# A delta-rule stage on pairs of heads: the identity added on VectorE, products spread over four array tiles, activation tables loaded at chosen places

## The chip, the core and the metric

The kernel runs on one core of one Trainium2 chip. The metric is the device time of one execution in microseconds (us), lower is better. TensorE (PE) does the matrix products and writes PSUM (eight banks of 128 partitions x 512 fp32), VectorE (DVE) and ScalarE (ACT) read PSUM, GpSimd (POOL) works on SBUF alone. Each engine has its own instruction queue; they meet at semaphores.

## The reference, cut to what matters

Two networks run one after the other: a two-layer block (Fourier mixing, then an RWKV-7 style mixer, each followed by an expert-choice mixture of experts) and a two-layer transformer. The change is about the RWKV scan of the first block (16 heads of 64, 512 tokens and 256 context tokens, forward and backward), and about where functions of ScalarE are used in all of the program.

```python
def wkv_scan(r, decay, k, v, a_vec, b_vec, s0, reverse):
    def step(s, inp):
        r_t, w_t, k_t, v_t, a_t, b_t = inp
        sa = jnp.einsum('bhvk,bhk->bhv', s, a_t)
        s = s * w_t[:, :, None, :] + sa[..., None] * b_t[:, :, None, :] + v_t[..., None] * k_t[:, :, None, :]
        return s, jnp.einsum('bhvk,bhk->bhv', s, r_t)
```

Around it: `a = sigmoid(...)`, `kk * rsqrt(sum(kk*kk) + 1e-12)`, `rsqrt(var + LNX_EPS)`, and in the norms `rsqrt(mean(h*h) + eps)`. The kernel writes each reciprocal root as Exp(-0.5 Ln(x)).

## The kernel before, in words

**The stage.** The heads are taken in eight pairs (`p`); a pair has two halves, one for each direction `d`. The 768 tokens are 12 chunks of 64 (`CH`), in three groups of four (`GC`, index `b`). Head one of the pair lies on partitions 0 to 63, head two on 64 to 127. `heads2` (line 1355) issues a product of 64x64 matrices for both heads; with `across=True` the result of each head goes to the other head's half of the partitions.

**The levels.** In every chunk the inverse of a triangular matrix is needed. It is doubled up in five levels. `X` holds the inverse so far and `XT` its transpose, side by side in one tile `XX`; POOL makes `NL`, the part of the triangular matrix that belongs to the level (line 3170). A level is: on TensorE `T` = product of `NL` and `X` (`level_t`, line 1433), which ScalarE copies to SBUF (`copied`, line 2046, all at line 2049); on TensorE the double product `XT`'`T` and `T`'`XT` into the two halves of one bank (`level_x`, line 1441); on VectorE X + (double product), 512 columns wide (`level`, line 2669, instruction at line 2675; in the last level only `XT`, line 2677).

**Beside the levels** runs what belongs to the other direction: a `chain` of 11 steps (named z; TensorE line 1450, VectorE line 2684) that carries the state from chunk to chunk, and on VectorE the preparation of the next half: a scan along the tokens (line 2691, and for one direction 2694), the keys (2700, 2705, 2707, 2710 or 2712), decays (2717, 2718, 2723, 2724, 2728), and for the output of the pair before 2748, 2753, 2759, 2764. ScalarE has the sigmoids (2068, 2069), the square (2059) and the scaling (2074) of the keys, Ln of the key sums (2079), the Exps (2089, 2098, 2114 to 2117). The sums over a head's channels (named kn, var, bonus) and the gate are 128-wide products at line 895.

**What sets the order.** Four lists, `RK_PE`, `RK_DVE`, `RK_ACT`, `RK_POOL`, name the steps of a pair in the order in which each engine does them; each finished step adds one to the engine's semaphore. `RK_READ` says which bank a step's result lies in and which step empties it. `banks` (line 1365) makes TensorE wait for the reader of the bank's last content. The loops of all four engines are written out in the same order. After the levels a half ends with scores, transposes, the products with the inverse and the chunk products (sb, sk, wu, ba, kt, ar, kv, bc, y), some of them with `across` products alternating with straight ones.

**Function tables.** ScalarE evaluates Ln, Exp, Sigmoid and Silu from tables that `ACT_TABLE_LOAD` brings in. The kernel of before leaves the loads to the compiler, which puts one ahead of each function whose table isn't in. `root` (line 1915, Ln at 1920, Exp at 1923) is used by every norm of the program.

Of the kernel before, what the change touches and what calls it, by code (L numbers as in the profile page):

```python
# [28 lines left out]
KT = D // 128  # L29
# [68 lines left out]
for _d in range(2):  # L98
# [4 lines left out]
    RK_PE += [("mv", _d, _b) for _b in range(3)] + [("kn", 0), ("kn", 1)] * _d  # L103
# [13 lines left out]
    for _l in range(1, 6):  # L117
        for _b in range(3):
            RK_DVE += [("XX", _d, _l, _b)] + [_z.pop(0) for _ in range(min(1, len(_z)))]
        RK_DVE += {1: [("scan", _a)] + [("kkn",)] * _d, 2: [("kdk", _a), ("bdk", _a), ("ksm", _a)] + [("yn",)] * _d,  # L120
                   3: [("ara", _a), ("arr", _a)],
                   4: [("bds", _a), ("kds", _a)] + ([("res1",), ("lnx",)] if _d else [("ksr",)]),
                   5: [("res",), ("bonus",)] * _d + [("mt", _a, 0)]}[_l]
# [5 lines left out]
    RK_ACT += [("mv", _d, _b) for _b in range(3)] + [("ka", _a)]  # L129
    for _l in range(1, 6):  # L130
        RK_ACT += [("T", _d, _l, _b) for _b in range(3)]
        RK_ACT += {1: [("kn", 0), ("kn", 1), ("var",), ("kr",), ("rs",)] * _d, 2: [("exps", _a)], 3: [("aff",)] * _d}.get(_l, [])
# [5 lines left out]

RK_READ = {}
_xx, _t, _a4 = 0, 0, 0  # L140
for _name in RK_PE:
# [4 lines left out]
    elif _k in ("x0", "XX"):  # L146
        RK_READ[_name] = {_xx % 2: [("dve", _name)]}
        _xx += 1
    elif _k in ("mv", "T"):
        RK_READ[_name] = {2 + _t % 2: [("act", _name)]}  # L150
        _t += 1
    elif _k == "z":
        RK_READ[_name] = {6: [("dve", _name)]} if _rest[1] < 11 else {}
        if _rest[1] == GC:
            RK_READ[_name][7] = [("dve", ("yf", _rest[0]))]
    elif _k in ("vt", "kn", "var", "bonus", "gate"):
        RK_READ[_name] = {4 + _a4 % 2: {"gate": [("dve", ("res",))], "bonus": [("dve", ("bonus",))]}.get(_k, [("act", _name)])}
        _a4 += 1
    elif _k == "mean":
        RK_READ[_name] = {0: [("dve", ("cen",))]}  # L160
    elif _k == "kv":
        RK_READ[_name] = {(1, 3, 4)[_rest[1]]: [("dve", ("bc",) + _rest)]}
        if _rest[1]:
            RK_READ[_name][(None, 2, 5)[_rest[1]]] = [("dve", ("y",) + _rest)]
    elif _k in ("bc", "y"):
        RK_READ[_name] = {}
    else:
        _bank = {"sb": (4, 4, 4), "sk": (5, 5, 5), "ba": (6, 6, 6), "kt": (7, 7, 7), "wu": (2, 3, 2), "ar": (0, 0, 1)}[_k][_rest[1]]
        RK_READ[_name] = {_bank: {"sb": [("act", ("nt",) + _rest)], "sk": [("dve", ("mt",) + _rest)], "ar": [("dve", _name)]}.get(_k, [("act", _name)])}
# [226 lines left out]
def build(nc, slabs_d, vecs_d, tabs1_d, tabs2_d, aux_d, lora_d, x_d, ctx_d, out_d, kv_d):  # L396
# [5 lines left out]
    with stack:  # L402
# [15 lines left out]
        P = [stack.enter_context(nc.psum_tensor(f"bank{i}", [128, 512], f32)) for i in range(8)]  # L418
# [471 lines left out]
        def _(pe):  # L890
# [474 lines left out]
            def banks(p, *name, after=()):  # L1365
# [3 lines left out]
                         if not (front and (step[0] in ("bonus", "res") or engine == "act" and step in RK_ACT[:RK_ACT.index(("pw", 0))])) and not (back and step[0] != "z")]  # L1369
# [63 lines left out]
            def level_t(p, d, l):  # L1433

                for b in range(3):
                    out, = banks(p, "T", d, l, b, after=[("pool", 0, "nl", d, l, b), ("dve", 0, "XX", d, l - 1, b) if l > 1 else ("dve", 0, "x0", d, b)])
                    for q, c in enumerate(chunks(b)):
                        m = heads2(out[:, q * CH:(q + 1) * CH], NL[:, c, :], X[:, c, :])
                    m.then_inc(rk_pe, rk.one("T", d, l, b))
# [43 lines left out]
            def inverse_times(p, d, b):  # L1483

                out, = banks(p, "wu", d, b, after=[("dve", 0, "XX", d, 5, b), ("act", 0, "mv", d, b)])
# [58 lines left out]
            for p in range(KT):  # L1544
                for d in range(2):
# [7 lines left out]
                    if d == 1:  # L1553
                        key_sums(p)
                    for l in range(1, 6):
                        level_t(p, d, l)
                        for b in range(3):
                            level_x(p, d, l, b)
                            if 3 * l + b < NCH + 2:
                                chain(p, a, 3 * l + b - 2)  # L1560
                        if (d, l) == (1, 1):
                            head_sums(p, "var", sqs, "act", ("sq",))
                            head_sums(p, "bonus", ksr, "dve", ("ksr",))
                        if (d, l) == (1, 2):
                            gate_product(p)
# [1841 lines left out]
```

## Time and profile before

| | us |
|---|---|
| median of 3 runs | 4458.05 |
| the runs | 4448.03 to 4460.98 |
| the profiled execution | 4450.12 |
| its span, first to last instruction | 4448.3 |
| of it the eight pairs (1227.8 to 2142) | 914 |

The share of the span that an engine is busy is an average over stages with different limits. The eight pairs are the stretch that the change is about; the rows that matter are taken from there, from one pair whose halves are 1345.3 to 1396.8 and 1396.8 to 1460.2 us. An instruction for TensorE of this program is two in the trace, since a product of fp32 matrices is made in two passes: a group of eight products is x16 there.

### The profile page before, as it was taken

What the parts mean: (1) busy time and instruction counts of PE and PEld (TensorE: products, weight loads), DVE (VectorE), ACT (ScalarE), POOL (GpSimd) and SP (SyncE); (2) the same over time, 40 slices, a digit from 0 to 9 for tenths busy, and PEclk for the clock granted to TensorE, in tenths of its full rate; (3) what the DMA queues carried; (4) which work ended last, traced back from release to release, by engine and by line L of the source; (5) the groups of instructions that cost most, each with busy time, mean ns of one, the idle gap of its engine ahead of it and who ended that gap; (6) DMA issues with size and microseconds to landing.
All of it is one profiled execution on the core that took longest, in us unless ns stands there. A gap on an engine that the chain in (4) does not pass through costs nothing.

```text
span 4448.3 us, 93542 instructions
## 1 busy us (share of the span) xinstructions
PE 4030.2 (91%) x40040; PEld 2621.0 (59%) x40040; DVE 1730.7 (39%) x3445; ACT 870.8 (20%) x1893; POOL 659.4 (15%) x603
## 2 busy tenths in 40 slices
PE   5989999989888888888879998999999989999998
PEld 4534444455477777777434443447588854657887
DVE  2412121164555555555231222354345424515353
ACT  2200000020144444444110001215000011330001
POOL 4000000000033333323000000000234300003342
PEclk8989999999999999999889999999999999999999
DMA  7387878832100000000249997110122221102221
GB/s 325 127 313 300 336 299 333 331 160 89 60 12 12 12 10 11 12 12 12 119 186 429 429 428 329 57 57 1 57 78 93 76 73 49 39 20 76 95 76 38
DMA packets 54241, 619.72 MB, mean 139 GB/s; under 512 B 5648, under 2 KB 8976, under 8 KB 18320
## 3 DMA queue, kind: packets, MB, share of 16 engines
q1 hardware_dynamic: 49664, 599.41, 34.1%
q10 hardware_dynamic: 2448, 9.05, 0.5%
q0 software_dynamic: 1792, 6.29, 0.4%
q8 instruction: 271, 4.44, 0.4%
q14 instruction: 66, 0.54, 0.0%
HBM read 602.40 MB, written 12.32 MB: 138 GB/s over the span
## 4 chain that ended last, share of the span: by engine, by line
PE 70%; issue 14%; DVE 6%; DMA 5%; ACT 1%; DVEq 1%; PEld 1%; PEldq 0%; SPq 0%; POOLq 0%; ACTq 0%; POOL 0%
PE bank L895 56%; PE bank L1358 13%; DMA ring<-slabs 3%; DMA work<-slabs 2%; DVE work L2675 1%; PEld bank L895 1%; DMA kv<-work 1%; PE bank L1405 1%; DVE hx L2367 0%; PEldq L1796 0%; DVE work L3049 0%; DVE work L2723 0%; DVE work L2724 0%; DVE work L2352 0%; DVE work L2343 0%
## 5 line engine op out<-in xcount | busy, mean ns | idle before, releaser
L895 PE MATMUL bank<-ring,work 128*32 128x256 f32 (+3 forms) x7002 | 764.4, 439 | 68.6 <-DMA ring<-slabs 56.7
L895 PE MATMUL bank<-work 128*128 128x256 f32 (+8 forms) x3590 | 783.0, 428 | 26.6 <-DVE work L3049 15.9
L895 PEld LDWEIGHTS bank<-work 128*128 128x128 f32 (+3 forms) x3590 | 498.2, 184 | 300.0 <-issue 219.5
L895 PEld LDWEIGHTS bank<-ring,work 128*32 128x32 f32 (+2 forms) x7002 | 317.2, 124 | 490.8 <-issue 387.1
L895 PE MATMUL bank<-work,ring 128*128 128x256 f32 (+1 forms) x1616 | 482.2, 456 | 14.7 <-DVE work L3068 5.1
L895 PE MATMUL bank<-hx,ring 128*128 128x512 f32 (+1 forms) x1344 | 485.7, 516 | 9.2 <-DVE hx L2367 7.3
L1358 PE MATMUL bank<-work 64*64 64x64 f32 x11520 | 419.5, 224 | 82.0 <-issue 62.6
L1358 PEld LDWEIGHTS bank<-work 64*64 64x64 f32 x11520 | 385.5, 139 | 118.2 <-issue 117.1
L895 PEld LDWEIGHTS bank<-work,ring 128*128 128x128 f32 x1616 | 306.6, 191 | 184.4 <-issue 134.4
L895 PEld LDWEIGHTS bank<-hx,ring 128*128 128x128 f32 x1344 | 257.1, 192 | 224.1 <-issue 200.4
L3186 POOL TENSOR_TENSOR work<-ring 128x512 f32<-128x512 f32 (+1 forms) x48 | 78.7, 1640 | 1938.0 <-DVE resc L3037 1490.2
L3170 POOL TENSOR_TENSOR work<-work,tabs_sb 128x256 f32<-128x256 f32 x288 | 226.0, 803 | 363.8 <-ACT work L2049 279.9
L2343 DVE TENSOR_TENSOR work<-work,bank 128x256 f32<-128x256 f32 x240 | 91.8, 416 | 405.7 <-ACT work L2321 402.2
L2049 ACT ACTIVATE work<-bank 128x256 f32<-128x256 f32 (+1 forms) x355 | 145.1, 416 | 372.8 <-PE bank L1358 367.7
L2675 DVE TENSOR_TENSOR work<-work,bank 128x512 f32<-128x512 f32 x192 | 131.4, 685 | 182.9 <-PE bank L1358 181.7
L2321 ACT ACTIVATE work<-bank 128x256 f32<-128x256 f32 x48 | 18.4, 383 | 735.0 <-PE bank L895 735.0
L1358 PE MATMUL bank<-ring,work 64*64 64x64 f32 (+1 forms) x3168 | 119.3, 258 | 40.6 <-issue 16.5
L895 PE MATMUL bank<-work,tabs_sb 128*128 128x512 f32 (+1 forms) x276 | 129.6, 598 | 14.5 <-ACT work L1907 9.5
L2560 DVE TENSOR_TENSOR work<-work,bank 128x256 f32<-128x256 f32 x16 | 6.8, 422 | 323.3 <-PE bank L895 323.3
L3049 DVE SCALAR_TENSOR_TENSOR work<-work 128x256 f32<-128x256 f32 x176 | 124.4, 722 | 14.7 <-issue 5.2
L1358 PEld LDWEIGHTS bank<-ring,work 64*64 64x64 f32 x3168 | 102.9, 144 | 46.2 <-issue 45.5
L895 PE MATMUL bank<-resc,work 128*128 128x256 f32 x512 | 121.3, 380 | 3.1 <-POOL work L3186 2.6
(315 smaller groups left out, 4621.8 us busy)
## 6 DMA issues: line engine op xcount, KB each, us to landing
ring<-slabs SPq DMA_DIRECT2D x228, 2048.0 KB, 9.7
work<-slabs SPq DMA_DIRECT2D x48, 2048.0 KB, 18.3
work<-kv SPq DMA_DIRECT2D x18, 384.0 KB, 3.0
kv<-work SPq DMA_DIRECT2D x2, 3072.0 KB, 15.7
kv<-work ACTq DMA_DIRECT2D x6, 512.0 KB, 17.2
work<-tabs ACTq DMA_DIRECT2D x1, 2176.0 KB, 9.5
resx<-xT SPq DMA_DIRECT2D x1, 2048.0 KB, 10.8
outT<-hx ACTq DMA_DIRECT2D x8, 256.0 KB, 2.6
```

What stands on the lines that cost most here:

```text
L895: return pe.matmul(out, lhsT, rhs, start=(k == 0), stop=(k == n - 1))
L1358: m = pe.matmul(out[other if across else r], lhsT[r], rhs[r], start=first, stop=last)
L1405: pe.matmul(outw[:, 0:n], wa2[two[d], 0:128], HW[two[d], at:at + n], start=True, stop=True)
L2049: act.activation(dst, src, ACT.Copy).then_inc(rk_act, rk.next(*name))
L2321: act.activation(keep1, ff_result(n, "p1"), ACT.Copy).then_inc(ff_act, 1)
L2343: v.tensor_tensor(out, a, b, op)
L2560: v.tensor_tensor(hidc, gactc[:, h, :], ex_bank(l, f"u{h}c")[:, 0:256], ALU.mult)
L2675: v.tensor_tensor(XX[:, :, cs_, :], XX[:, :, cs_, :], p4, ALU.add).then_inc(rk_dve, rk.one("XX", d, l, b))
L3049: return v.scalar_tensor_tensor(dst, x, 1.0, y, ALU.mult, ALU.subtract)
L3170: m = pool.tensor_tensor(NL[:, cs_, :], NT[d][:, cs_, :], mask, ALU.mult)
L3186: pool.tensor_tensor(s3, a["a11"], a["a21"], ALU.subtract).then_inc(ff_pool, 1)
```

## The change

1. **Levels.** VectorE adds the identity to `T` as it takes it out of PSUM (256 columns). The double product is then the new `X` and `XT` itself, not what is to be added, and ScalarE copies it out, both halves in one instruction of 512 columns. The two halves of the double product lie in two banks (a pair of banks 0 and 1, or 4 and 5), and one of the two products is issued `across`, so that they go to different array tiles.
2. **Order within a level.** Before: T0 T1 T2, XX0 z XX1 z XX2 z. After: T0 T1 z T2, XX0 z XX1 XX2 z on TensorE, and T0 T1 z T2 z (first part of the other work) z (second part) on VectorE.
3. **Other places.** The sums kn and var stand ahead of level 1, gate and bonus behind level 4. Ln of the keys and of the variance stands ahead of the level loop; the scaling of the keys stands behind level 1.
4. **Tables.** `preload_act_table_set` names a set with both Ln and Exp, and sets for sigmoid and for silu, at chosen places.
5. **Banks.** A new table `RK_BANK`, and one PSUM tensor for all eight banks, so that one instruction can read two.

```diff
-    for _l in range(1, 6):
-        RK_PE += [("T", _d, _l, _b) for _b in range(3)]
-        for _b in range(3):
-            RK_PE += [("XX", _d, _l, _b)] + [_z.pop(0) for _ in range(min(1, len(_z)))]
-        RK_PE += {1: [("var",), ("bonus",)], 2: [("gate",)]}.get(_l, []) * _d
+    for _l in range(1, 6):
+        RK_PE += [("T", _d, _l, 0), ("T", _d, _l, 1)] + [_z.pop(0) for _ in range(min(1, len(_z)))] + [("T", _d, _l, 2)]
+        RK_PE += [("XX", _d, _l, 0)] + [_z.pop(0) for _ in range(min(1, len(_z)))] + [("XX", _d, _l, 1), ("XX", _d, _l, 2)]
+        RK_PE += [_z.pop(0) for _ in range(min(1, len(_z)))]
+        RK_PE += [("gate",), ("bonus",)] * (_d == 1 and _l == 4)
...
+    elif _k == "XX":
+        _pair = 4 * (_rest[2] % 2)
+        RK_READ[_name] = {_pair: [("act", _name)], _pair + 1: [("act", _name)]} if _rest[1] < 5 else {(0, 4, 1)[_rest[2]]: [("act", _name)]}
...
-                out, = banks(p, "XX", d, l, b, after=[("act", 0, "T", d, l, b)])
+                outs = banks(p, "XX", d, l, b, after=[("dve", 0, "T", d, l, b)])
                 for q, c in enumerate(chunks(b)):
                     if l < 5:
-                        heads2(out[:, q * CH:(q + 1) * CH], XT[:, c, :], T[d][:, c, :])
-                    m = heads2(out[:, 256 + q * CH:256 + (q + 1) * CH], T[d][:, c, :], XT[:, c, :])
+                        heads2(outs[0][:, q * CH:(q + 1) * CH], XT[:, c, :], T[d][:, c, :], across=l > 1)
+                    m = heads2(outs[-1][:, q * CH:(q + 1) * CH], T[d][:, c, :], XT[:, c, :], across=l in (1, 5))
...
+            def level_copy(p, d, l, b):
+
+                cs_ = slice(GC * b, GC * b + GC)
+                if l < 5:
+                    pair = list(RK_READ["XX", d, l, b])[0]
+                    copied(p, XX[:, :, cs_, :], PB[:, pair:pair + 2, 0:256].rearrange("p x (c n) -> p x c n", c=GC), "XX", d, l, b)
+                else:
+                    copied(p, XT[:, cs_, :], ONE(rk_bank("XX", d, l, b)[:, 0:256]), "XX", d, l, b)
...
-                v.wait_ge(*rk_done("pe", p, "XX", d, l, b))
-                p4 = rk_bank("XX", d, l, b)[:, :].rearrange("p (x c n) -> p x c n", x=2, c=GC)
-                cs_ = slice(GC * b, GC * b + GC)
-                if l < 5:
-                    v.tensor_tensor(XX[:, :, cs_, :], XX[:, :, cs_, :], p4, ALU.add).then_inc(rk_dve, rk.one("XX", d, l, b))
-                else:
-                    v.tensor_tensor(XT[:, cs_, :], XT[:, cs_, :], p4[:, 1, :, :], ALU.add).then_inc(rk_dve, rk.one("XX", d, l, b))
+                v.wait_ge(*rk_done("pe", p, "T", d, l, b))
+                v.tensor_tensor(T[d][:, GC * b:GC * b + GC, :], rk_bank("T", d, l, b)[:, 0:256].rearrange(CHUNKED, c=GC),
+                                bc(eye2.unsqueeze(1), 128, GC, CH), ALU.add).then_inc(rk_dve, rk.one("T", d, l, b))
...
                     for b in range(3):
                         copied(p, AM[d][:, GC * b:GC * b + GC, CH:128], ONE(rk_bank("mv", d, b)[:, 0:256]), "mv", d, b)
-                    key_factors(p, a)
+                    act.preload_act_table_set("natural_log_exp_and_others")
+                    if d == 1:
+                        key_logs(p)
+                        variance_logs(p)
...
+                    if p < KT - 1 or d == 0:
+                        act.preload_act_table_set("sigmoid_and_others")
```

The order on TensorE, first in one level of a half (behind the first T groups of level 2; `resc` and `work` are the chain's operands, x2 the two products of a z step, `work` alone T and XX). Before:

```order
L1358 MATMUL bank<-work 64x64 x40
L1358 MATMUL bank<-resc,work 64x64 x2
L1358 MATMUL bank<-work,resc 64x64 x2
L1358 MATMUL bank<-work 64x64 x16
L1358 MATMUL bank<-resc,work 64x64 x2
L1358 MATMUL bank<-work,resc 64x64 x2
L1358 MATMUL bank<-work 64x64 x16
```

After:

```order
L1353 MATMUL bank<-work 64x64 x16
L1353 MATMUL bank<-resc,work 64x64 x2
L1353 MATMUL bank<-work,resc 64x64 x2
L1353 MATMUL bank<-work 64x64 x24
L1353 MATMUL bank<-resc,work 64x64 x2
L1353 MATMUL bank<-work,resc 64x64 x2
L1353 MATMUL bank<-work 64x64 x32
```

The first z step stands between the second and the third T group now, and the last two double products stand together.

VectorE in levels 1 and 2 of a second half (`d` = 1). Before:

```order
L2675 TENSOR_TENSOR work<-work,bank 128x2x256
L2684 SCALAR_TENSOR_TENSOR work<-bank,work,hc 128x64
L2691 SCALAR_TENSOR_TENSOR work<-tabs_sb,work 128x780
L2700 SCALAR_TENSOR_TENSOR work<-work 128x768
L2675 TENSOR_TENSOR work<-work,bank 128x2x256
L2684 SCALAR_TENSOR_TENSOR work<-bank,work,hc 128x64
```

After:

```order
L2694 TENSOR_TENSOR work<-bank,tabs_sb 128x256
L2702 SCALAR_TENSOR_TENSOR work<-bank,work,hc 128x64
L2709 SCALAR_TENSOR_TENSOR work<-tabs_sb,work 128x780
L2702 SCALAR_TENSOR_TENSOR work<-bank,work,hc 128x64
L2718 SCALAR_TENSOR_TENSOR work<-work 128x768
L2694 TENSOR_TENSOR work<-bank,tabs_sb 128x256 x2
```

The 512-wide additions have become 256-wide ones, and a chain step stands between the two parts of the other work.

ScalarE at the start of the same half, from the copies of mv on. Before:

```order
L2049 ACTIVATE ring<-bank 128x4x64 x3
L2074 ACTIVATE work<-work 128x768
L2049 ACTIVATE work<-bank 128x256 x3
L2079 ACT_TABLE_LOAD
L2079 ACTIVATE work<-bank,work 128x256
L2079 ACTIVATE work<-bank,work 128x512 x2
L2089 ACT_TABLE_LOAD
L2089 ACTIVATE work<-work 128x768
L2098 ACTIVATE work<-work 128x512
L2049 ACTIVATE work<-bank 128x256 x3
```

After:

```order
L2054 ACTIVATE ring<-bank 128x4x64 x3
L2172 ACT_TABLE_LOAD
L2084 ACTIVATE work<-bank,work 128x256
L2084 ACTIVATE work<-bank,work 128x512 x2
L2054 ACTIVATE work<-bank 128x2x256 x3
L2079 ACTIVATE work<-work 128x768
L2094 ACTIVATE work<-work 128x768
L2103 ACTIVATE work<-work 128x512
L2054 ACTIVATE work<-bank 128x2x256 x3
```

The load and the three Lns stand ahead of the level's first copies, the second load is gone, and the copies are 512 wide.

## Rows read from the trace of the kernel before

**Rows 1.** Page, part 1: engine, busy us, share, instructions.

```profile
PE 4030.2 (91%) x40040; PEld 2621.0 (59%) x40040; DVE 1730.7 (39%) x3445; ACT 870.8 (20%) x1893; POOL 659.4 (15%) x603
```

**Rows 2.** Windows of two halves and five pairs: length, busy us by engine, clock.

```profile
1345.30:1396.80 51.50, 43.99 (x1382) 40.11 (x1378) 30.30 (x60) 20.73 (x44) 17.85 (x24) 1.00 0.05 14
1396.80:1460.20 63.40, 52.00 (x1438) 45.90 (x1434) 30.96 (x60) 27.03 (x53) 16.34 (x24) 0.95 0.03 10
1460.20:2031.50 571.30, 477.24 (x14064) 429.56 (x14060) 304.87 (x600) 239.16 (x486) 171.71 (x231) 0.96 0.04 12
```

**Rows 3.** Timeline of TensorE, first half: start, duration, tiles, idle before.

```profile
1348.93 0.98 PE L1358 MATMUL bank<-work 64*64 64x64 f32 x32 [1.48 <-issue]
...
1377.76 0.27 PE L1358 MATMUL bank<-ring,work 64*64 64x64 f32 x2
```

**Rows 4.** Timeline of TensorE, second half.

```profile
1403.39 2.83 PE L1358 MATMUL bank<-work 64*64 64x64 f32 x80
...
1413.78 2.70 PE L1358 MATMUL bank<-work 64*64 64x64 f32 x48 [1.83 <-issue]
...
1435.64 0.68 PE L1358 MATMUL bank<-work 64*64 64x64 f32 x16 [1.01 <-DVE work L2677]
1438.13 1.18 PE L1358 MATMUL bank<-ring,work 64*64 64x64 f32 x27 [1.80 <-DVE work L2764]
```

**Rows 5.** TensorE: a z product, a double product, and straight with across alternating.

```profile
1423.36 0.31 PE L1358 MATMUL bank<-work,hc 64*64 64x64 f32 x4
1423.48 1.13 PE L1358 MATMUL bank<-work 64*64 64x64 f32 x32
...
1391.32 0.69 PE L1358 MATMUL bank<-work,hx 64*64 64x64 f32 x32 [1.42 <-issue]
```

**Rows 6.** Groups of instructions of the eight pairs: busy us, mean ns, idle before.

```profile
L2675 DVE TENSOR_TENSOR work<-work,bank 128x512 f32<-128x512 f32 x192 | 131.4, 685 | 182.9 <-PE bank L1358 181.7
L2684 DVE SCALAR_TENSOR_TENSOR work<-bank,work,hc 128x64 f32<-128x64 f32 x80 | 22.2, 278 | 0.7 <-PE bank L1358 0.7
L2666 DVE TENSOR_TENSOR work<-bank,tabs_sb 128x256 f32<-128x256 f32 x47 | 19.9, 424 | 34.2 <-PE bank L1358 33.6
L2707 DVE TENSOR_TENSOR work<-work 128x768 f32<-128x768 f32 x16 | 18.8, 1175 | 0.0
L2705 DVE TENSOR_TENSOR work<-work 128x768 f32<-128x768 f32 x16 | 15.2, 948 | 0.0
```

**Rows 7.** VectorE's other work in levels 1 to 4, by half.

```profile
1356.14:1359.10 2.96, 2.89 (x4) 1.00 0.02 6
1362.63:1365.87 3.24, 3.24 (x5) 1.00 0.00 0
1369.11:1371.02 1.91, 1.91 (x3) 1.00 0.00 0
1374.38:1376.79 2.41, 2.41 (x5) 1.00 0.04 7
...
1420.12:1423.70 3.58, 3.58 (x6) 1.00 0.02 5
1426.93:1428.97 2.04, 2.00 (x3) 1.00 0.04 8
1432.68:1435.08 2.40, 2.40 (x5) 1.00 0.03 7
```

**Rows 8.** Timeline of ScalarE: two loads of a table, one 512-wide copy.

```profile
1345.26 1.28 ACT L2068 ACT_TABLE_LOAD   x1 [1.00 <-PE bank L1406]
...
1410.76 1.28 ACT L2089 ACT_TABLE_LOAD   x1
...
1441.16 0.60 ACT L2049 ACTIVATE work<-bank 128x512 f32<-128x512 f32 x1 [1.32 <-PE bank L1358]
```

**Rows 9.** Line 1923: count, duration in ns min/median/max, first and last start.

```profile
L1923 ACT ACT_TABLE_LOAD  x10: 1283/1283/1283, 47.0 to 4437.8; - x10
```

**Rows 10.** Window behind the wait at 1438: busy us, granted clock.

```profile
1437.90:1441.20 3.30, 3.07 (x59) 3.08 (x61) 0.51 (x2) 0.43 (x2) 0.00 (x0) 0.50 0.44 144
```

More of the change, by code:

```diff
@@ L24 @@
 from contextlib import ExitStack, contextmanager
+import itertools
 import math
@@ L136 @@
     RK_POOL += [("nl", _d, _l, _b) for _l in range(6) for _b in range(3)] + [("qm", _a, 1), ("qm", _a, 2)]
+RK_BANK = {"vt": (0, 1), "x0": (2, 3, 2), "mv": (0, 1, 0), "kn": (4, 5), "var": (7,), "T": (2, 3, 2), "gate": (7,), "bonus": (6,), "mean": (6,),
+           "sb": (4, 4, 4), "sk": (5, 5, 5), "ba": (0, 0, 0), "kt": (1, 1, 1), "wu": (2, 3, 2), "ar": (6, 6, 5)}
 RK_READ = {}
-_xx, _t, _a4 = 0, 0, 0
 for _name in RK_PE:
@@ L155 @@
             RK_READ[_name][7] = [("dve", ("yf", _rest[0]))]
[L156 to L160, printed above, removed]
     elif _k == "kv":
-        RK_READ[_name] = {(1, 3, 4)[_rest[1]]: [("dve", ("bc",) + _rest)]}
+        RK_READ[_name] = {(7, 3, 7)[_rest[1]]: [("dve", ("bc",) + _rest)]}
         if _rest[1]:
-            RK_READ[_name][(None, 2, 5)[_rest[1]]] = [("dve", ("y",) + _rest)]
+            RK_READ[_name][(None, 2, 4)[_rest[1]]] = [("dve", ("y",) + _rest)]
     elif _k in ("bc", "y"):
@@ L167 @@
     else:
-        _bank = {"sb": (4, 4, 4), "sk": (5, 5, 5), "ba": (6, 6, 6), "kt": (7, 7, 7), "wu": (2, 3, 2), "ar": (0, 0, 1)}[_k][_rest[1]]
-        RK_READ[_name] = {_bank: {"sb": [("act", ("nt",) + _rest)], "sk": [("dve", ("mt",) + _rest)], "ar": [("dve", _name)]}.get(_k, [("act", _name)])}
+        _by = {"sb": ("act", ("nt",) + _rest), "sk": ("dve", ("mt",) + _rest), "mean": ("dve", ("cen",)), "gate": ("dve", ("res",))}
+        _by.update({_q: ("dve", _name) for _q in ("x0", "T", "ar", "bonus")})
+        RK_READ[_name] = {RK_BANK[_k][_rest[-1] if _rest else 0]: [_by.get(_k, ("act", _name))]}
 RK_FREE, _last = {}, {}
@@ L417, in build @@
         work = sb("work", [128, WORK])
-        P = [stack.enter_context(nc.psum_tensor(f"bank{i}", [128, 512], f32)) for i in range(8)]
+        PB = stack.enter_context(nc.psum_tensor("bank", [128, 8, 512], f32))
+        P = [PB[:, i, :] for i in range(8)]
         slab_loaded = [sem(f"slab_loaded{s}") for s in range(2 * RING)]
@@ L1368, in banks @@
                 freed = [(engine, before) + step for steps in RK_FREE[name].values() for engine, step, before in steps
-                         if not (front and (step[0] in ("bonus", "res") or engine == "act" and step in RK_ACT[:RK_ACT.index(("pw", 0))])) and not (back and step[0] != "z")]
+                         if not (front and (step[0] in ("bonus", "res", "XX") or engine == "act" and step in RK_ACT[:RK_ACT.index(("pw", 0))])) and not (back and step[0] != "z")]
                 for engine in ("dve", "act", "pool"):
@@ L1483, in inverse_times @@
             def inverse_times(p, d, b):
-                out, = banks(p, "wu", d, b, after=[("dve", 0, "XX", d, 5, b), ("act", 0, "mv", d, b)])
+                out, = banks(p, "wu", d, b, after=[("act", 0, "XX", d, 5, b), ("act", 0, "mv", d, b)])
                 for q, c in enumerate(chunks(b)):
@@ L1554, in _ @@
                         key_sums(p)
+                        head_sums(p, "var", sqs, "act", ("sq",))
+                    steps = iter(range(1, NCH))
                     for l in range(1, 6):
[L1556 to L1562, printed above, removed]
+                        level_t(p, d, l, 0)
+                        level_t(p, d, l, 1)
+                        for j in itertools.islice(steps, 1):
+                            chain(p, a, j)
+                        level_t(p, d, l, 2)
+                        level_x(p, d, l, 0)
+                        for j in itertools.islice(steps, 1):
+                            chain(p, a, j)
+                        level_x(p, d, l, 1)
+                        level_x(p, d, l, 2)
+                        for j in itertools.islice(steps, 1):
+                            chain(p, a, j)
+                        if (d, l) == (1, 4):
+                            gate_product(p)
                             head_sums(p, "bonus", ksr, "dve", ("ksr",))
-                        if (d, l) == (1, 2):
-                            gate_product(p)
                     scores(p, a, 0)
```

101 lines of the change are left out of this document (59 added, 42 removed).

## The prediction

> **What bounds the kernel now.** First the page: TensorE is busy for 91% of the span, so what shortens another engine pays only where TensorE waits for it [rows 1]. Then windows: a pair takes 51.5 + 63.4 us, and the next five pairs take 571.3, 114.3 each; TensorE is idle for 7.5 and 11.4 us of the two halves [rows 2]. Then its timeline. In the first half, T of level 1 starts at 1349.4 (behind the 16 products of mv in the merged row) and the scores at 1377.76: 28.4 us for five levels [rows 3]. In the second it is 1403.39 to 1438.13: 34.7 us, with waits of 1.83, 1.01 and 1.80 us [rows 4]. A level is one loop: T, its copy, the double product, the addition on VectorE, T of the next level. TensorE's own work in a level, from the repeating rows: T 3 x 0.47, double products 3 x 0.95, z 3 x 0.24, sum 5.0. So the levels that last 5.5 us are TensorE's, and those of 6 to 10 us are set by VectorE or ScalarE, whose other work lies ahead of the addition or the copy.
>
> **Part 1, the double product on four tiles.** 32 instructions of the double product last 1.13 us with their pipeline; 32 of the kind in which straight and `across` products alternate last 0.69. Less the 0.22 of the last one, that is 0.93 against 0.48 of issue [rows 5]. The changed product has that second form, so I take 0.48. TensorE's work in a level falls to 1.4 + 1.4 + 0.7 = 3.55 us. The last level has single products and keeps its 0.47 each.
> What speaks against it is a rule of the Trainium skill. In TensorE: Matmul & The Clock Gate, section "Wait — 56ns, not 53.3ns?", matmuls never start closer than about 25 ns however small they are. By that rule a double product would take 0.80 us at best; the alternating row, with about 15 ns from start to start, disagrees, and the row decides.
>
> **Part 2, additions and copies.** VectorE's three additions of 0.685 us become three of 0.424, the form of line 2666 [rows 6]: 0.8 us less a level. ScalarE's three copies become 512 wide. One from a single bank takes 0.60 us [rows 8]; from two banks there is no row. The bounds are 0.60 and twice a 256-wide copy (0.76); I take 0.60. Three of them fit into a level either way.
>
> **Part 3, one level after.** I count from the start of the third T group. TensorE does T2 and XX0 (0.95), z (0.24, and 0.22 until its end), VectorE's chain step ends 0.2 to 0.28 later: 1.6 us. Here the other work begins. Behind it stand the third chain step (0.22) and the addition to T0 of the next level (0.42, and 0.1 until TensorE goes on; T2 needs T0's bank). So a level lasts 2.34 us plus the other work, and not under 3.84, which is TensorE's 3.55 and a wait for the copy of XX0, whose banks XX2 needs. In level 4 the second z is the 512-wide sum and there is no third: 2.5 plus the other work.
> First half, other work 2.96, 3.24, 1.91, 2.41 [rows 7]: levels of 5.3, 5.6, 4.25, 4.9, sum 20.0. Ahead of the first count lie 1.24 us (T0, T1, z), behind the last 2.15 (XX of level 5, its copy, then the scores). 23.4 us instead of 28.4: **5.0 less**.
> Second half: in level 1 the normed keys wait for ScalarE's Exp, which stands behind the copies and the scaling. Two 768-wide steps of about 0.95 (an estimate: 0.60 scaled from 512 to 768 columns) behind the copy that ends 3.2 us in, then 1.0 on VectorE: 6.5. Level 2: 2.34 + 3.58 = 5.9. Level 3: 2.34 + 2.04 = 4.4. Level 4: gate and bonus, two 512-wide products of 0.96, now stand at its end: 5.5. Sum 22.3, with both ends 25.7 instead of 34.7: **9.0 less**. Gone are the 1.83 us in which T of level 2 waited for a copy behind Ln, load and Exp, and the two waits at the end, for the bank that bonus filled. What is late next is the level's first addition, behind the keys.
>
> **Part 4, tables.** The sigmoid load (1.28, [rows 8]) stands ahead of the sigmoids, mv's third group waits for them (1.48 idle in [rows 3]). It goes to the end of the half before, where ScalarE waits for TensorE for some microseconds: 1.3 less in the first half. In the second var (0.96) moves into the same place: 0.35 less. The new load behind the copies of mv is hidden under T and XX of level 1: I count 0.8 us to spare in the first half, and 1.3 with the three Lns in the second; without that cover each would cost up to 1.28.
> The page also has ten loads of 1.28 between Ln and Exp of a norm [rows 9], at which VectorE waits for the Exp. The first lies under the load of weights; nine go, 11.5 us. Ahead of the pairs and behind them lines 2079, 2089 and 2098 have four more; the scaling of the keys takes the gain of one: I count 4.1.
> The Trainium skill (ScalarE: Activation LUTs, section "What ACT_TABLE_LOAD costs") gives 2.66 us for a switch, 1.38 of it a drain. By the page the outer gain would be twice as much, some 15 us more; in the rows nothing stands between load and Exp, so the sum goes by 1.28.
>
> **Part 5, clock and sharing.** Behind the wait at 1438 TensorE ran at half clock for 3.3 us [rows 10]. With that wait gone I count 1.0 us of it back. New waits of 1.5 to 2 us in the DVE-bound levels can bring other such stretches, and GpSimd's masks now run beside denser VectorE work (line 2707 takes 1.18 us where its like, 2705, takes 0.95 [rows 6]). I take 0.8 us a pair off for both. The bank table costs nothing: the pairs of banks wait for readers that are done, but for the 0.3 us in XX2 counted above.
>
> **The sum.** A pair: 5.0 + 9.0 + 1.3 + 0.35 + 1.0 - 0.8 = 15.85; eight: 127. Outside: 11.5 + 4.1 = 15.6. Together 143. The profiled execution had 4450.1 us, so 4307 by its own time; the median of the three runs lies 8 us higher, so **4315** by that, which I take.
>
> **The rivals.**
> *A: the double product doesn't get to 0.48.* The tile pairs are new for operands that VectorE and ScalarE wrote just before. At 0.93 a level lasts 2.8 us plus the other work: half a microsecond more in each of eight levels, 4 a pair, 32 in all: 4347. Against it stand the alternating rows. By the 25 ns of the skill's page above it would be 0.33 us a level, 21 in all: 4336.
> *B: sharing between VectorE and GpSimd.* If all the other work stretched as line 2707 does against 2705 (24%), the 21 us of it in a pair would cost 5 more: 41 in all, 4356. For it speaks that the masks of the next level start with VectorE's additions now; against it that the windows of [rows 7] have some of it already.
> *C: slower than before, by the clock.* TensorE has less to do in a level and waits once in each. If the levels ran at half clock throughout, T, XX and z would take 6.6 us a level and the chain of 2.34 about 3.6; with both ends some 22 us a pair more than forecast, 176 in all: 4490. It decides once four fifths of the levels ran so. Against it: the halves had 1.00 and 0.95 of the clock [rows 2], the dips stand behind waits of 1.8 us, and those go.
> *D: the tables don't do what is said.* The compiler might add loads for Exp or Sigmoid all the same. The order shows four loads a pair for five, and none between Ln and Exp; if they cost more where they stand (both covers gone, 2.6 a pair), 21: 4336.
>
> **How the numbers follow.** Forecast 0.70, from 4280 (levels half a microsecond shorter each, which takes 32 us off) to 4345; A 0.09, B 0.13, C 0.03, D 0.05. The range should hold 8 in 10: from 4275 to 4370, with A, B and D alone in it. A measurement of this kernel can tell about 0.3% from no change, 13 us. All but C and a sum of several rivals are faster by more: 0.95; within it 0.02; slower 0.03.
>
> **What the profile after would show.** Double products as x32 rows of 0.7 us, or x64 of 1.2 where two stand together. Levels of 4.3 to 6.5 us, the second half's level 1 the longest, waiting for VectorE's first addition. Halves of 45 and 52 us. No 1.8 us wait at level 2 or before the scores. Four loads of a table in a pair, and none between Ln and Exp. Wrong would be: double products at 1.13 (A), other work over 3.5 us in level 2 (B), a clock of 0.8 in the pairs (C), ScalarE late with the first copies of level 1 (D).

## The result, and the profile after

The changed kernel takes 4386.71 us, median of 4 runs (4374.17 to 4399.33), against 4455.51 for the kernel before: a ratio of 0.9837 with an interval of 0.9816 to 0.9857. A second set of six runs gave 0.9832 (0.9809 to 0.9856). The forecast was 4315 with a range from 4275 to 4370: the sign was right, the gain was 69 us where 143 were expected, and the time lies outside of the range.

The profiled execution was the slowest of the four, 4399.33. Part 1 of its page, to be held against [rows 1]:

```profile
PE 3938.0 (90%) x40040; PEld 2527.7 (57%) x40040; DVE 1677.7 (38%) x3445; ACT 851.6 (19%) x1847; POOL 614.9 (14%) x603
```

The eight pairs in one window, of before and then of after (length, busy us of TensorE, its weight loads, VectorE, ScalarE, GpSimd, then clock and DMA):

```profile
1226.40:2144.90 918.50, 763.65 (x22439) 685.43 (x22436) 487.23 (x956) 381.99 (x776) 272.63 (x365) 0.96 0.04 12
```

```profile
1242.00:2103.80 861.80, 664.60 (x22442) 585.02 (x22436) 427.26 (x957) 409.84 (x767) 228.06 (x365) 0.95 0.05 13
```

TensorE's work fell by 99 us, as much as was counted on, but the stretch fell by 57 only: its idle time rose from 155 to 197 us. A pair takes 107.7 us instead of 114.8. Two halves and the five pairs behind them, as in [rows 2]:

```profile
1350.90:1402.00 51.10, 38.73 (x1379) 35.12 (x1379) 26.21 (x58) 23.51 (x45) 14.39 (x23) 0.97 0.05 14
1402.00:1460.10 58.10, 43.88 (x1440) 37.80 (x1438) 27.39 (x63) 27.79 (x51) 14.41 (x23) 0.94 0.04 11
1460.10:1997.00 536.90, 418.09 (x14067) 367.14 (x14064) 267.25 (x600) 257.69 (x482) 143.98 (x230) 0.95 0.04 13
```

The idle time has no owner that the profile names. In the same stretches, what TensorE waited for longest in total (us in total, times, longest), before and after:

```profile
PE bank L1358 <- issue: 109.5, 108, 2.6
```

```profile
PE bank L1353 <- issue: 154.2, 149, 2.3
```

"issue" is a wait for nothing that the profile shows. The chain that ended last, in the levels of one second half of after:

```profile
1417.27 1.02 DVE work L2718
1418.28 0.34 DVE work L2694
1418.63 0.14 issue
1418.76 1.88 PE bank L1353 x63
1420.64 1.75 issue
1422.39 2.22 PE bank L1353 x69
```

Between the waits that a reader expects (VectorE's addition, line 2694) stand such of 1 to 2 us in the middle of TensorE's own work. One of them from close by, with its two neighbours in TensorE's timeline:

```profile
1477.04 0.56 PE L1353 MATMUL bank<-work 64*64 64x64 f32 x21
...
1479.59 0.82 PE L1353 MATMUL bank<-work 64*64 64x64 f32 x38 [1.99 <-issue]
```

And what the DMA engines did from 1476 to 1484, in 40 slices of 0.2 us:

```profile
DMA  0000030000000000000000000000300000000000
...
q8 instruction: 2, 0.03, 1.9%
```

Two packets of 16384 B of TensorE's instructions, the first at 1477.11. TensorE stands still 0.3 us later and goes on 2.5 us after the packet began. This is a pattern: I took from the instruction records of the eight pairs all waits of TensorE over 0.6 us (from the start of one matrix instruction to the start of the next), and counted those that end 2.1 to 2.9 us after a packet began. I call these late packets. Before there are 60 among 122 such waits, 81 us in all; after 119 among 156, 169 us. The number of packets is 181 in both. If packets and waits had nothing to do with each other, the 181 windows of 0.8 us would catch some 19 and 26. In the five levels alone, from the first T to the scores, late packets cost 2.3 us a pair before and 13.3 after.

### The profile page after: what moved, and what is told of

Its sections match the earlier page's. It is cut to its first block, busy times and chain, and to the rows that moved or that the text cites. A ratio compares the mean times of both kernels' runs of the same rounds, so it can differ in the third digit from the quotient of the medians.

```text
span 4397.5 us, 93458 instructions
## 1 busy us (share of the span) xinstructions
PE 3938.0 (90%) x40040; PEld 2527.7 (57%) x40040; DVE 1677.7 (38%) x3445; ACT 851.6 (19%) x1847; POOL 614.9 (14%) x603
## 4 chain that ended last, share of the span: by engine, by line
PE 70%; issue 15%; DMA 5%; DVE 5%; ACT 1%; DVEq 1%; PEld 1%; PEldq 0%; SPq 0%; POOLq 0%; POOL 0%; ACTq 0%
PE bank L890 57%; PE bank L1353 12%; DMA ring<-slabs 2%; DMA work<-slabs 2%; PEld bank L890 1%; DMA kv<-work 1%; PE bank L1400 1%; DVE hx L2389 0%; PEldq L1797 0%; DVE work L3091 0%; DVE work L2694 0%; DVE work L2374 0%; DVE work L2365 0%; DVE work L3110 0%; DVE hc L2434 0%
## 5 line engine op out<-in xcount | busy, mean ns | idle before, releaser
L1353 PE MATMUL bank<-work 64*64 64x64 f32 x11520 | 338.4, 235 | 119.6 <-issue 82.6
L1353 PEld LDWEIGHTS bank<-work 64*64 64x64 f32 x11520 | 309.4, 146 | 155.0 <-issue 151.7
L2054 ACT ACTIVATE work<-bank 128x512 f32<-128x512 f32 (+1 forms) x355 | 186.2, 532 | 319.3 <-PE bank L1353 315.3
L3212 POOL TENSOR_TENSOR work<-work,tabs_sb 128x256 f32<-128x256 f32 x288 | 181.3, 641 | 342.9 <-DVE work L2694 258.6
L2694 DVE TENSOR_TENSOR work<-bank,tabs_sb 128x256 f32<-128x256 f32 x240 | 97.7, 421 | 109.2 <-PE bank L1353 107.2
L890 PE MATMUL bank<-hx,work 128*128 128x256 f32 x512 | 121.2, 380 | 0.4 <-POOL work L3229 0.4
```

The source lines that it names most:

```text
L890: return pe.matmul(out, lhsT, rhs, start=(k == 0), stop=(k == n - 1))
L1353: m = pe.matmul(out[other if across else r], lhsT[r], rhs[r], start=first, stop=last)
L2054: act.activation(dst, src, ACT.Copy).then_inc(rk_act, rk.next(*name))
L2694: v.tensor_tensor(T[d][:, GC * b:GC * b + GC, :], rk_bank("T", d, l, b)[:, 0:256].rearrange(CHUNKED, c=GC), bc(eye2.unsqueeze(1), 128, GC, ...
L3212: m = pool.tensor_tensor(NL[:, cs_, :], NT[d][:, cs_, :], mask, ALU.mult)
```

## The experiments

All ratios are to the kernel before, run beside each. "Pairs" is the stretch of the eight pairs in the profiled execution. The counts of late packets are good to two or three. The run burst isn't in the table: it was executed once (4587.82 us) for its trace alone.

| run | ratio (interval) | pairs, us | packets | late packets |
|---|---|---|---|---|
| before | 1 | 918.5 | 181 | 60, 81 us |
| changed kernel | 0.9837 (0.9816 to 0.9857) | 861.8 | 181 | 119, 169 us |
| after_again | 0.9832 (0.9809 to 0.9856) | 878.0 | 181 | 116, 174 us |
| two_tiles | 0.9833 (0.9810 to 0.9857) | 869.3 | 181 | 109, 143 us |
| wide_levels | 0.9708 (0.9684 to 0.9733) | 813.3 | 139 | 73, 106 us |
| before_wide | 0.9951 (0.9933 to 0.9970) | 894.5 | 140 | 46, 68 us |
| no_preload | 0.9939 (0.9918 to 0.9960) | 904.6 | 181 | 112, 159 us |
| tables_alone | 0.9916 (0.9897 to 0.9934) | 909.5 | 181 | 63, 84 us |
| gate_late | 0.9804 (0.9785 to 0.9823) | 859.0 | 181 | 106, 154 us |
| pool_wait | 0.9807 (0.9787 to 0.9828) | 882.8 | 181 | 116, 176 us |
| transposes | 1.0311 (1.0288 to 1.0334) | 1062.0 | 174 | 63, 93 us |
| transposes_late | 1.0312 (1.0295 to 1.0328) | 1050.2 | 174 | 54, 84 us |
| improved | 0.9782 (0.9756 to 0.9808) | 843.8 | 181 | 112, 156 us |

**after_again**, the changed kernel once more.

> The changed kernel once more, as the base for the runs beside it: 4387 us give or take 10, that is 65 to 75 us less than before. TensorE's instructions come in packets of 16384 B (in the trace of the changed kernel 181 of them while the eight pairs run). Theory F (fetch): TensorE's unexplained waits end 2.1 to 2.9 us after such a packet starts; in the changed kernel there are 116 such waits with 164 us in all, in the kernel before 60 with 81 us. I expect the same counts within 10% here. The rival L (the levels' other work on VectorE and ScalarE is longer than I counted) expects nothing of this run.

4396.63 us (4376.73 to 4416.49), late packets as before. The same program's pairs took 861.8 and 878.0 us: single profiles of it differ by 16 us there, and only the ratios of many runs decide below.

**burst**: the changed kernel with products ahead of the pairs that have nothing to wait for.

```diff
+            for _i in range(64):
+                row4(0)          # 4 x (straight pair, across pair)
+            for _i in range(64):
+                row2(2)          # the same number, all straight
+            for _i in range(32):
+                wide4(4)         # 128 columns, alternating
+            with pe.Fori(0, 16) as _i:
+                for _j in range(4):
+                    row4(6)
```

> Ahead of the pairs TensorE has, with nothing to wait for: 1024 products of 64x64 (2048 instructions in the trace) written out, straight and across alternating; 1024 written out, all straight; 512 of 128 columns alternating; and a loop of 16 rounds with 64 alternating products each. Theory F: the first stretch can't keep its 15 ns: it takes one packet (about 118 instructions of this kind) in about 3.3 us, 27 ns each, some 57 us; the second 29 ns each, 59 us, nearly the same; the third as long as its columns need, 1024 instructions in 30 us or a little more; the loop, whose instructions need no new packet, keeps 15 to 17 ns in a round. If fetching were no limit, the first stretch would take 31 us.

The four stretches as windows:

```profile
1212.10:1270.20 58.10, 33.56 (x2048) 31.51 (x2051) 3.51 (x16) 0.02 (x1) 0.00 (x0) 1.00 0.02 5
1270.20:1331.35 61.15, 61.05 (x2058) 60.86 (x2052) 0.00 (x0) 0.00 (x0) 0.00 (x0) 0.98 0.02 4
1331.35:1359.90 28.55, 28.53 (x1033) 28.07 (x1033) 0.00 (x0) 0.00 (x0) 0.00 (x0) 1.00 0.02 5
1359.90:1393.30 33.40, 32.79 (x2057) 31.46 (x2049) 0.00 (x0) 0.00 (x0) 0.00 (x0) 1.00 0.00 0
```

Rows from TensorE's timeline in the first stretch:

```profile
1215.87 2.09 PE L1353 MATMUL bank<-tabs_sb 64*64 64x64 f32 x128 [1.15 <-issue]
1219.88 2.09 PE L1353 MATMUL bank<-tabs_sb 64*64 64x64 f32 x128 [1.92 <-issue]
1223.89 2.09 PE L1353 MATMUL bank<-tabs_sb 64*64 64x64 f32 x128 [1.92 <-issue]
```

This is the mechanism alone. 128 matrix instructions (64 products, two instructions each) and their 128 weight loads are one packet, 64 B for each; TensorE starts them every 15 ns and then stands for 1.2 to 1.9 us. The packets begin 3.3 to 4.5 us apart, 3.6 on average (58.1 us for 16): 28 ns for each matrix instruction, where two tiles take 30 and have no waits. The loop of the same products, whose instructions are fetched once (one packet in its window against 16), takes 33.4 us instead of 58.1. The gain of the four tiles is real for one packet and nearly nothing over several, 58.1 us against 61.2.

The Trainium skill (Runtime: NRT & Kernel Launch, section "Instruction fetch mechanics") gives the blocks of 16 KiB and 256 instructions, and this trace agrees. It also says that fetching is hidden, since the sequencer issues more slowly than blocks arrive; the stretch at 58.1 us contradicts that for 64-column products.

**two_tiles**: the first product for all four chunks, then the second.

```diff
                 for q, c in enumerate(chunks(b)):
                     if l < 5:
                         heads2(outs[0][:, q * CH:(q + 1) * CH], XT[:, c, :], T[d][:, c, :], across=l > 1)
+                for q, c in enumerate(chunks(b)):
                     m = heads2(outs[-1][:, q * CH:(q + 1) * CH], T[d][:, c, :], XT[:, c, :], across=l in (1, 5))
```

> Only the order in a double product is changed: first the four chunks of one product, then those of the other, so that products come on two array tiles at a time, and 32 of them should take 0.93 us instead of 0.48. Theory F: TensorE can't be fed faster than one packet of instructions in about 3.3 us anyway, so the waits for packets shrink by most of what the products grow: the time stays within 10 us of the changed kernel, and the sum of waits falls from 164 to under 130 us. Rival L, and the working of the prediction (half a microsecond in each of eight levels of a pair): 32 us more than the changed kernel.

```profile
1226.70:2096.00 869.30, 693.00 (x22439) 616.94 (x22434) 420.53 (x957) 411.58 (x767) 227.93 (x365) 0.97 0.05 13
```

TensorE is busy for 28 us more than in the changed kernel, and the time is the same (0.9833). The waits for packets shrink by 26 us, less than I expected (143 us, not under 130). The clock has a part in it too: by the prediction's 0.93 and 0.48 the 192 double products should have added 86 us of busy time, but two_tiles spent 48 us of the pairs at half clock (granted 0.50) where the changed kernel spent 85 and, in after_again, 96. No run holds the clock fixed, so how the equal time divides between packets and clock is open. Either way the four tiles, the change's most expensive part in banks, bring nothing here.

**wide_levels**, and the same in the kernel before, **before_wide**:

```diff
-                for q, c in enumerate(chunks(b)):
-                    m = heads2(out[:, q * CH:(q + 1) * CH], NL[:, c, :], X[:, c, :], across=l > 1)
+                for q, c in list(enumerate(chunks(b)))[::2]:
+                    m = heads2(PAIR(out, q), NL[:, c, :], X[:, c:c + 2, :], across=l > 1)
```

and alike for both halves of the double product.

> In the levels one product of 128 columns stands for two of 64 (both chunks with the first one's weights, so the inverse is not computed and what follows is not the reference's): TensorE passes as many columns, with half the instructions. Theory F: about 670 of a pair's 2670 matrix instructions go, so the packets of the pairs fall from 181 to about 136, the waits for them from 164 us to under 90, and the time by 50 to 80 us, to about 4320. Rival L (VectorE's and ScalarE's other work sets the levels): the time stays within 15 us of the changed kernel.

> The kernel before, with the same edit in its levels as wide_levels: one product of 128 columns stands for two of 64 (second chunks get the first one's weights, the inverse is not computed). Theory F: its levels bring 32 double products in 0.93 us and wait for VectorE's 512-wide additions between, so packets are seldom late in them; the packets of the pairs fall from 181 to about 139, the waits for them from 81 us to about 50, and the time by 15 to 35 us, half of what the same edit gave in the changed kernel (63 us). If the number of instructions cost the same in both kernels: 60 us.

```profile
1227.20:2040.50 813.30, 633.49 (x17065) 539.63 (x17060) 428.55 (x957) 407.68 (x767) 228.30 (x365) 0.97 0.05 13
```

Both kernels give every second chunk the first one's weights, so they don't compute the inverse and serve as measurements alone. The same columns in fewer instructions make the changed kernel 63 us faster (4333.91 against 4396.63) and the one before 22 (4441.14 against 4463.53). Both as theory F had it; the rival, that VectorE and ScalarE set the levels, allowed 15. But not all of it is packets. In burst a 128-column instruction on four tiles starts every 27.3 ns and two of 64 columns take 29.2; on two tiles it is 54.6 ns in before_wide against 58.3. By the count of products (an estimate from these rows) TensorE's own work gets 14 us shorter in the changed kernel and 19 in the one before. That leaves some 49 us for the packets in the changed kernel and little in the one before, where few came late in the levels. The levels of a pair shrink from 28.1 + 30.6 us to 24.9 + 27.2 (means of eight, first T to scores). So of the 4.7 and 4.9 us by which they exceeded the forecast of 23.4 and 25.7, 3.2 and 3.4 went with the instructions, some 0.9 of each being own work. What is left over, 1.5 each, is not taken apart; 73 late packets are still in the pairs.

**no_preload** and **tables_alone**: the change without its nine lines on tables, and these lines alone in the kernel before.

```diff
-                    act.preload_act_table_set("natural_log_exp_and_others")
+                    pass
```

> The changed kernel without its nine lines that name a table: the compiler places the loads again. By the prediction's terms the changed kernel loses what the tables gave it: 15.6 us outside of the pairs, and the load ahead of the sigmoids (1.3) in eight first halves, 10 us: 26 us slower than the changed kernel. By the trace after (10 to 13 us gained outside of the pairs, behind them) 20 to 24 us slower. If the loads never lay on the path: within 5 us of it.

> The kernel before, with the nine lines that name a table put in where the changed kernel has them, and nothing else of the change: ScalarE's order, the levels, the products and the banks are those of before. The loads outside of the pairs and the one between Ln and Exp in a second half go, the one ahead of the sigmoids moves to the end of the half before. no_preload showed that the changed kernel loses 42 to 50 us without these lines. If they are worth as much by themselves, this kernel takes 4415 us, 40 to 50 less than before, and the levels' part of the change is worth only some 25. By the prediction's terms: 15.6 outside and 8 x 1.3 at the sigmoids, 26 us less than before.

4438.77 and 4430.41 us. Without the lines the changed kernel loses 42 us against after_again (48 by the two ratios), far over the 20 to 26 expected; the lines alone give 37 us (expected 40 to 50, or 26 by the prediction's terms). More than half of the gain is the tables; the levels, products and banks together are worth some 25 us (4463.53 less 4438.77), where the prediction had 117. Why they are worth more in the changed kernel than I priced them, in ScalarE's timeline of no_preload and then of the changed kernel, at the same place of a second half:

```profile
1413.37 1.28 ACT L2084 ACT_TABLE_LOAD   x1
...
1423.84 1.28 ACT L2094 ACT_TABLE_LOAD   x1
1425.13 0.84 ACT L2094 ACTIVATE work<-work 128x768 f32<-128x768 f32 x1
```

```profile
1407.74 1.28 ACT L2172 ACT_TABLE_LOAD   x1
1409.04 1.63 ACT L2084 ACTIVATE work<-bank,work 128x256 f32<-128x256 f32 x3
...
1415.48 1.02 ACT L2079 ACTIVATE work<-work 128x768 f32<-128x768 f32 x1
1416.40 0.83 ACT L2094 ACTIVATE work<-work 128x768 f32<-128x768 f32 x1
```

The second load of no_preload stands ahead of the Exp for which the keys on VectorE wait, and behind those the level's first addition. Up to the first T the second half is 2.7 us longer, and levels 1 and 2 together by 1.6 (medians). I had put this load into the second half's 9.0 us and not priced it apart.

**transposes** and **transposes_late**: half of the products with the identity as true transposes, one instruction each instead of two.

```diff
-                return heads2(out, in_, eye2, across=across)
+                for r, other in (two, two[::-1]):
+                    to = other if across else r
+                    m = pe.transpose(out[to], in_[r], eye2[r]) if to is two[0] else pe.matmul(out[to], in_[r], eye2[r], start=True, stop=True)
+                return m
```

> The changed kernel, exact in its result: those transposes (product with the identity) whose result goes to the lower 64 partitions are issued as transposes, which are one matrix instruction instead of two. 84 of the 2804 matrix instructions of a pair go, with their weight loads: 3% of the stream, 0.7 of 22.6 packets a pair. Theory F, at 2.0 to 2.4 us for a packet, as wide_levels had it (62 us for 42 packets is 1.5 us for each, TensorE's time being equal): 8 to 13 us less than the changed kernel. A rival that counts only TensorE's own time (84 x 15 to 29 ns a pair, most of it beside waits): 5 us or less.

> The kernel of the run transposes, and the gate and bonus products stand behind level 5's last product instead of behind level 4. There TensorE waits 0.9 us for the copy of it anyway, and no level waits behind them: level 4 of each second half gets 1.9 us shorter, the end of level 5 about 1.0 longer: another 0.9 a pair, 7 us less than transposes. If VectorE's multiplications behind them (0.7 us each) then come late for the first mask of the scores, the gain is gone: same as transposes.

4600.34 us, 137 slower than the kernel before. There were fewer packets and fewer late ones than in the changed kernel, as expected, but that was drowned by something that I had not thought of. The products with the identity of the eight pairs by group, in the changed kernel and then in transposes:

```profile
L1353 PE MATMUL bank<-tabs_sb,work 64*64 64x64 f32 x2634 | 93.8, 228 | 10.7 <-issue 10.7
```

```profile
L1360 PE MATMUL bank<-tabs_sb,work 64*64 64x64 f32 x1970 | 300.7, 259 | 2.9 <-issue 2.9
```

A quarter fewer instructions, three times the busy time, 26 us a pair. The mean of one is hardly longer (0.26 us), so it is their overlap that is lost: at full clock starts are 0.11 us apart on average instead of 0.03. And the clock fell: 266 us of the pairs ran at half clock, where the starts are 0.19 apart, against 85 in the changed kernel. It looks as if a transpose waited for the products before it, and they for it, but no run shows what they wait for. transposes_late came out equal and says nothing of the gate's place.

**gate_late**, **pool_wait**, **improved**: edits of order.

```diff
-        RK_PE += [("gate",), ("bonus",)] * (_d == 1 and _l == 4)
+        RK_PE += [("gate",), ("bonus",)] * (_d == 1 and _l == 5)
...
+            pool.wait_ge(norm_dve, 8)
             for half in range(2):
```

> The changed kernel; gate and bonus products stand behind level 5's last product instead of behind level 4. Level 4 of a second half (8.0 us) gets 1.9 us shorter; at the end of level 5, where TensorE waits 0.9 us for a copy, 1.0 to 1.9 are added. Gain up to 0.9 us a pair, 7 us or less; if packets of instructions come late at the new place as at the old one, none. The run transposes_late against transposes (1 us) speaks for little.

> The changed kernel; far ahead of the pairs, GpSimd waits with its four additions of 2048 columns (4.55 us each) until VectorE has scaled hc, 16 small instructions of 0.3 us of which two or four take 4.6 us when they run beside GpSimd (two in the traces of before, two_tiles, wide_levels; four in those of the changed kernel twice). Theory P (the two engines share a port, so which of the two states comes is a matter of a microsecond, and this is where the changed kernel's profiled executions lost 12 us ahead of the pairs): no instruction of VectorE there over 1 us, TensorE's instruction 1000 at 124 us or earlier instead of 137, executions that differ less, median 5 to 15 us below the changed kernel. The rival (GpSimd's sums are needed in time too): TensorE waits for them later, no gain.

> The changed kernel with three edits of order: gate and bonus behind level 5 (as in gate_late), GpSimd waiting for VectorE's 16 small instructions (as in pool_wait), and the first of all lora products no longer waiting for VectorE's memsets ahead of the pairs (in the trace after it waits there until 1213.1; nothing has read its banks by then). The three are apart in time, so they should add: 5 to 13 us, up to 12 and 3 us, 10 to 20 together, a ratio to the kernel before of 0.978 to 0.981. Its stream of instructions is as long as that of the changed kernel, so theory F leaves the pairs' 181 packets and some 105 to 116 late ones, and this kernel far from the 4315 of the prediction.

gate_late gives 4383.65 and pool_wait 4388.13 us, both some 0.3% better in ratio than the changed kernel, with intervals that overlap its own. In gate_late level 4 of a second half went from 8.0 to 6.1 us, but what follows became 2.6 longer, so its gain isn't explained by the place. All three edits together give 4364.39 us and a ratio of 0.9782, its interval just clear of the changed kernel's two (0.9808 against 0.9809 and 0.9816): the fastest kernel here that computes the reference's result, 0.5% below the changed one. How it divides among the three isn't settled; the third, by the distance of TensorE's instructions 8000 and 8400, is worth 1.4 us.

What pool_wait removes, VectorE and then TensorE in the changed kernel, and GpSimd in pool_wait:

```profile
91.68 0.34 DVE L2434 TENSOR_SCALAR hc<-hc,work,mod 128x128 f32<-128x128 f32 x1
...
101.28 4.61 DVE L2434 TENSOR_SCALAR hc<-hc,work,mod 128x128 f32<-128x128 f32 x1
105.81 4.58 DVE L2435 TENSOR_SCALAR hc<-hc,work 128x127 f32<-128x127 f32 x1
```

```profile
110.78 5.27 PE L890 MATMUL bank<-ring,hx 128*128 128x129 f32 x24 [9.84 <-DVE work L2443]
```

```profile
91.94 4.53 POOL L3160 TENSOR_TENSOR work<-ring 128x2048 f32<-128x2048 f32 x1 [4.44 <-DVE hc L2435]
```

An instruction of VectorE that takes 0.34 us by itself takes 4.6 when GpSimd runs a 4.5 us addition. Four fell into this in the changed kernel's profile, two in that of the kernel before: 12.3 us by TensorE's instruction 1000 (137.4 against 125.1 us), at a place that the change doesn't touch. The changed kernel's two profiles both have four, and so have gate_late and no_preload; two_tiles and wide_levels, whose edits come only behind that place, have two: the change doesn't force it. The three profiles without the change's new order (before, before_wide, tables_alone) have two each, which is too few to say whether it makes it likelier. In pool_wait none was over 1 us and instruction 1000 stood at 123.8. Its executions still differ by 30 us, so this is at most a part of their spread.

## Why the prediction was wrong

**Part 1, the double product at 0.48: the step that failed.** As a row it was right; after has them as x32 of 0.69, and burst starts 128 at 15 ns each. What failed is "TensorE's work in a level falls to 3.55 us" as a bound that a level can reach. TensorE needs one packet for 128 matrix instructions and gets one in 3.2 us at the very best, in burst in 3.6 on average. A pair's 2804 of them are 22.6 packets, at 3.6 us 81 us of its 107.7: where products were made faster, TensorE uses up what lies ready and stands. The row was there: the wait of 1.42 us ahead of the alternating products in [rows 5] ends 2.6 us after a packet began (1388.73). I read waits put down to issue as waits for a copy or a bank, one by one, and never asked what they have in common.

**Part 2, additions and copies: right.** By form, in the eight pairs of after:

```profile
L2054 ACT ACTIVATE work<-bank 128x512 f32<-128x512 f32 x248 | 146.3, 597 | 246.3 <-PE bank L1353 244.7
L2694 DVE TENSOR_TENSOR work<-bank,tabs_sb 128x256 f32<-128x256 f32 x240 | 97.7, 421 | 109.2 <-PE bank L1353 107.2
L2723 DVE TENSOR_TENSOR work<-work 128x768 f32<-128x768 f32 x16 | 16.2, 1014 | 0.0
```

A copy from two banks takes 0.60, the value taken; the additions 0.42.

**Part 3, the levels: the mis-sized term.** Forecast 23.4 and 25.7 us from the first T to the scores, measured 28.1 and 30.6, where before had 29.0 and 34.7 (means of eight). 5.0 us gained a pair instead of 14.0, times eight 72 us short: as much as the whole miss. In the levels late packets cost 13.3 us a pair where before had 2.3, 11.0 more, which is enough for the 9.0 that are missing; the other waits over 0.6 us there fell, from 65 to 39 us in all eight pairs. The single waits named were right: that of 1.83 us at level 2 and those of 1.80 and 1.01 before the scores are gone, and what came late next in the second half was VectorE's first addition behind the keys, as the chain above shows. It fell into level 2 (8.5 us by the distance of the T groups, 4.6 for level 1), and both together, 13.0, are close to the 12.4 forecast. Levels 3 and 4 there were to take 9.9 and took 13.7. Not all of that is packets: by the prediction's own 2.5 plus 2.4 level 4 takes 4.9 without gate and bonus, so its 5.5 has only 0.6 for these two products of 0.96 each; gate_late shows the level 1.9 us shorter without them.

**Part 4, tables: right in place, too small in price.** First half 1.27 us shorter ahead of the levels (forecast 1.3), second 0.42 (0.35), the new load covered. Behind the pairs 9.7 us were gained. Ahead of them 15.6 were lost in this profile: 12.3 by VectorE beside GpSimd, 3.3 at the first lora products, which by the new bank table wait for VectorE's memsets. In improved, without that wait, 1.4 of the 3.3 came back; the others aren't explained. On the 2.66 us for a switch of the Trainium skill (ScalarE: Activation LUTs, section "What ACT_TABLE_LOAD costs"): in no_preload, too, the Exp follows the load by 0.01 us, with no drain between.

**Part 5, clock: wrong sign.** I had a gain of 1.0 and a loss of 0.8 a pair. The time at half clock within the pairs rose from 65 to 85 us (96 in after_again). Of the 17 stretches at half clock 8 stand behind a wait of 2 us or more for a packet and 5 behind one for VectorE's first addition in level 2 of a second half.

**The rivals.** B's 4356 comes nearest in time to the 4387, by a mechanism that wasn't at work: line 2723 takes 1.01 us, less than the 1.18 of line 2707 before, and GpSimd's masks 0.64 (0.80 before). A, 4347, fell since the products did reach 0.48, and two_tiles gives that up and loses nothing. C fell with a clock of 0.95. D fell: 40 loads as the order showed, none at an uncovered place. The range was too narrow since all four rivals took TensorE's stream for given.

## What to carry to other kernels

Before a product is made shorter, divide TensorE's instructions in the stretch by the time that is hoped for. Here a packet of 128 matrix instructions and 128 weight loads took 3.2 us at best and 3.6 on average, so written-out instructions shorter than some 28 ns gain next to nothing over more than a packet; fewer and wider ones do, and in burst so does a loop. And when waits put down to issue grow as a kernel gets faster, lay them beside the instruction queue's transfers before giving each its own cause.

## What the runs showed of the hardware

- Instruction packets: 16384 B, 128 matrix instructions with their loads; TensorE goes on 2.1 to 2.9 us after one begins, though its transfer takes 1.0 us; back to back they begin 3.3 to 4.5 us apart, 3.6 on average.
- Matrix instructions of 64x64 on four tiles: 15 ns from start to start, 16.3 in a loop over 2048 of them.
- Transposes mixed with ordinary products lose the overlap, 300.7 us for 1970 instructions instead of 93.8 for 2634, and the pairs spend 266 us at half clock instead of 85.
- VectorE beside GpSimd: 0.34 us became 4.6, and in the changed kernel's profile four in a row did, beside four additions of GpSimd. The Trainium skill (SBUF — State Buffer, section "Who interferes with whom") has this as an exclusive lock on a shared port; the rows agree.
